# Head norm and gate of the RWKV half, and the first block of the output projection: roots and reciprocals in columns

## The reference, cut to what matters

```
def rwkv_output(y, f, lp):
    mean = jnp.mean(y, axis=-1, keepdims=True)              # over the 64 channels of a head
    var = jnp.mean(jnp.square(y - mean), axis=-1, keepdims=True)
    yn = ((y - mean) * lax.rsqrt(var + GN_EPS)).reshape(y.shape[:2] + (RWKV_WIDTH,))
    yn = yn * lp['ln_w'] + lp['ln_b']
    bonus = sum(jnp.sum(f['r'] * kd * lp['rk'], axis=-1, keepdims=True) * f['v'] for kd in f['k'])
    return (yn + bonus.reshape(yn.shape)) * f['gate']       # f['gate'] = sigmoid(g) @ g2
...
out_l = jnp.concatenate([att_l, rw_l.astype(att_l.dtype)], axis=-1) @ lp['w_out']
```

## Time and profile before

| what | value |
|---|---|
| median of 3 executions | 1767.23 us (1766.62 to 1778.11) |
| profiled execution, its own time | 1766.91 us |
| its span, first to last instruction | 1765.1 us |
| mean granted TensorE clock | 0.942 of full speed |
| PE busy | 1607.1 us (91%) |
| DVE, ACT, POOL busy | 715.8, 569.9, 860.7 us (41%, 32%, 49%) |

### The profile page before, as it was taken

The page is one execution under the profiler, slowest core; times in us unless marked ns, Lnnn a source line. Parts: engine busy times, 40 slices in busy tenths (PEclk is TensorE's granted clock), DMA queues, the critical chain, the costliest instruction groups (busy, mean ns, idle before and its releaser), DMA issues. The chain is left out here.

```text
span 1765.1 us, 35427 instructions
## 1 busy us (share of the span) xinstructions
PE 1607.1 (91%) x15584; PEld 1321.9 (75%) x15584; DVE 715.8 (41%) x1060; ACT 569.9 (32%) x816; POOL 860.7 (49%) x399
## 2 busy tenths in 40 slices
PE   5899999588888886789999999999989899999996
PEld 2688878467676784678888888888867688888885
DVE  2343256667686755652121212640194521212135
ACT  3424245543435323233232313032221432323230
POOL 1432100296867741526778888834442344444441
PEclk9999999788999998889999999969999799999998
DMA  8321100031312221223444444212221122222221
GB/s 324 131 73 48 57 1 1 1 112 62 122 52 99 75 76 57 70 72 119 145 146 148 149 148 145 95 48 95 95 95 48 48 95 96 96 95 95 95 95 48
DMA packets 23617, 162.15 MB, mean 92 GB/s; under 512 B 2624, under 2 KB 3264, under 8 KB 4800
## 3 DMA queue, kind: packets, MB, share of 16 engines
q1 hardware_dynamic: 21904, 154.09, 24.4%
q10 hardware_dynamic: 1584, 6.13, 0.9%
HBM read 157.71 MB, written 2.10 MB: 91 GB/s over the span
## 5 line engine op out<-in xcount | busy, mean ns | idle before, releaser
L221 POOL TENSOR_TENSOR v<-raw,v 128x1024 fp32r<-128x1024 f32 x160 | 388.3, 2448 | 422.3 <-ACT v L209 397.9
L238 PE MATMUL bank<-hm,v 128*128 128x512 f32 x2112 | 488.2, 393 | 7.9 <-DVE hm L1852 5.4
L238 PEld LDWEIGHTS bank<-hm,v 128*128 128x128 f32 x2112 | 399.3, 190 | 97.1 <-issue 10.6
L238 PE MATMUL bank<-hid,v 128*128 128x512 f32 x1536 | 349.5, 389 | 0.0
L238 PEld LDWEIGHTS bank<-hid,v 128*128 128x128 f32 x1536 | 288.3, 188 | 59.9
L209 ACT ACTIVATE v<-raw 128x2048 fp32r<-128x2048 f32 x77 | 147.5, 1916 | 421.0 <-PE bank L238 420.9
L1983 DVE TENSOR_TENSOR bank<-bank,rl 128x512 f32<-128x512 f32 x64 | 44.8, 700 | 275.2 <-ACT rl L1962 275.2
L221 POOL TENSOR_TENSOR w<-raw,w 128x1024 fp32r<-128x1024 f32 x22 | 54.1, 2478 | 136.2 <-ACT w L209 136.2
L937 POOL TENSOR_TENSOR raw<-raw,cs 128x2048 f32<-128x2048 f32 x24 | 87.6, 3650 | 52.1 <-DVE at L1383 52.1
L511 PE MATMUL bank<-h,w 128*128 128x512 f32 x600 | 109.3, 344 | 0.0
L511 PEld LDWEIGHTS bank<-h,w 128*128 128x128 f32 x600 | 94.0, 191 | 14.3 <-issue 0.3
(11 more groups left out here) (288 smaller groups left out, 2349.3 us busy)
## 6 DMA issues: line engine op xcount, KB each, us to landing
raw<-w_in SPq DMA_DIRECT2D x119, 1024.0 KB, 4.8
mraw<-wm_in SPq DMA_DIRECT2D x16, 1024.0 KB, 4.8
raw<-wm_in SPq DMA_DIRECT2D x3, 1024.0 KB, 16.3
xres<-x_in ACTq DMA_DIRECT2D x1, 2048.0 KB, 8.2
yb<-wm_in SPq DMA_DIRECT2D x2, 1024.0 KB, 19.5
mixed_in<-wm_in SPq DMA_DIRECT2D x2, 1024.0 KB, 23.3
xres<-x_in SPq DMA_DIRECT2D x1, 2048.0 KB, 7.5
out_T<-xres ACTq DMA_DIRECT2D x8, 256.0 KB, 2.0
```

What stands on the lines that cost most here:

```text
L221: i = nc.gpsimd.tensor_tensor(W[1][n % 2][:, k:k + 4], raw[n % 2][:, k:k + 4], W[0][n % 2][:, k:k + 4].bitcast(F32), SUB)
L238: last = nc.tensor.matmul(bank(b(s, m), 0, hi - lo), W[w][s][:, k, m * P:(m + 1) * P], H[h][:, k, lo:hi], start=(k == 0 and w == h == 0), ...
```

## The change

- The sums of squares are made per token in columns: for each pair and each group of 128 tokens, the squares are the stationary operand and two columns of onesh the moving one. 16 such matmuls write a 128x32 piece of PSUM, gsum (tokens on partitions). One ACT root and one DVE reciprocal of 128x32 follow, ginv.
- ginv is spread back over the channels by 32 matmuls of 64 stationary columns (a broadcast column of ginv) with the identity as moving operand, 8 per pair, two halves of 64 output partitions.
- The gate's matmuls stand before the sums of squares. DVE multiplies weight and gate into the centred values (yg) and offset and gate into the bonus (in vT) beforehand, and afterwards does one product and one sum per pair. The ACT step L1588 is gone.
- g2 is loaded at the end of the block before, behind the load of x, and lies in a buffer of its own.
- ACT makes W[0] of block 35 and h[0] of the attention half first in the block; W[0] of block 36 follows the root.
- W[1] of block 36 is made by DVE, in one instruction after its last sum, and no longer by POOL.
- The product of block 35 goes over k outside and the two tiles m inside.

```diff
...
+    g2 = sb(drw, "g2", [P, PAIRS * P])
...
             sp.dma_start(x[:], A["x"]).then_inc(x_back, 16)
+            sp.dma_start(g2[:], A["g2"]).then_inc(g2_in, 16)
...
-                for i in range(PAIRS):
-                    pe.wait_ge(gsq_ready, i + 1)
-                    nc.tensor.matmul(bank(i), K("onesh"), sq[i % 2][:], start=True, stop=True).then_inc(var_done, 1)
                 pe.wait_ge(g2_in, 16)
                 for i in range(PAIRS):
                     nc.tensor.matmul(bank(4 + i), g2[:, i * P:(i + 1) * P], gT[:], start=True, stop=True)\
                         .then_inc(gate_done, 1)
-
-                pe.wait_ge(root_ready, PAIRS)
-                pe_block(pe, S_OUT, W, h, parts=one,
-                         ready=lambda k: (lo_made, max(1, k - PAIRS + 2)))
+                for i in range(PAIRS):
+                    pe.wait_ge(gsq_ready, i + 1)
+                    for g in range(TG):
+                        at = 2 * (i * TG + g)
+                        last = nc.tensor.matmul(gsum[:, at:at + 2], sq[i][:, g * P:(g + 1) * P], K("onesh")[:, ::HD],
+                                                start=True, stop=True)
+                last.then_inc(gsum_done, 1)
+                pe.wait_ge(ginv_ready, 1)
+                for i in range(PAIRS):
+                    if i >= 2:
+                        pe.wait_ge(gated, 2 * (i - 1))
+                    for g in range(TG):
+                        for e in range(2):
+                            last = nc.tensor.matmul(spread_at[i][e * HD:(e + 1) * HD, g * P:(g + 1) * P],
+                                                    ginv[:, i * TG + g, e:e + 1].to_broadcast([P, HD]), K("ident"),
+                                                    start=True, stop=True)
+                    last.then_inc(spread_done, 1)
+
+                s = S_OUT % 2
+                pe.wait_ge(split_ready[s], nth(S_OUT))
...
+                for k in range(KT):
+                    pe.wait_ge(lo_made, max(1, k - PAIRS + 2))
+                    for m in range(2):
+                        for w, e in ((0, 0), (0, 1), (1, 0)):
+                            last = nc.tensor.matmul(bank(2 * s + m), W[w][s][:, k, m * P:(m + 1) * P], h[e][:, k, :],
+                                                    start=k == w == e == 0, stop=(k == KT - 1 and w == 1))
...
             def _(act):
+                act_hi(act, S_OUT, W)
+                nc.scalar.activation(h[0][:, 0:PAIRS, :], attT, ACT.Copy).then_inc(hi_made, 1)
                 for i in range(PAIRS):
                     act.wait_ge(yc_ready, i + 1)
...
+                    nc.scalar.activation(sq[i][:], rT[:, i, :], ACT.Square).then_inc(gsq_ready, 1)
+                act.wait_ge(gsum_done, 1)
+                nc.scalar.activation(flat, gsum, ACT.Sqrt, bias=small[:, 1:2], scale=1.0 / HD).then_inc(root_ready, 1)
                 act_hi(act, S_OUT + 1, W)
...
             def _(dve):
...
+                    nc.vector.scalar_tensor_tensor(yg[i][:], rT[:, i, :], R("lnw", i, i + 1), bank(4 + i), MUL, MUL)\
+                        .then_inc(gated, 1)
+                    nc.vector.scalar_tensor_tensor(vT[:, i, C:N], vT[:, i, C:N], R("lnb", i, i + 1), bank(4 + i), ADD, MUL)\
+                        .then_inc(gated, 1)
+                    if i == 2:
+                        dve.wait_ge(root_ready, 1)
+                        nc.vector.reciprocal(flat, flat).then_inc(ginv_ready, 1)
+                dve.wait_ge(gsq_ready, PAIRS)
+                for i in range(PAIRS + 1):
+                    if i < PAIRS:
+                        dve.wait_ge(spread_done, i + 1)
+                        dve.wait_ge(gated, 2 * i + 2)
+                        nc.vector.tensor_tensor(spread_at[i], spread_at[i], yg[i][:], MUL).then_inc(yn_ready, 1)
+                    if i:
+                        dve.wait_ge(yn_ready, i)
+                        nc.vector.tensor_tensor(rT[:, i - 1, :], spread_at[i - 1], vT[:, i - 1, C:N], ADD)\
+                            .then_inc(o_ready, 1)
+                dve.wait_ge(hi_ready[(S_OUT + 1) % 2], nth(S_OUT + 1))
+                s = (S_OUT + 1) % 2
+                nc.vector.tensor_tensor(W[1][s][:], raw[s][:], W[0][s][:].bitcast(F32), SUB).then_inc(split_ready[s], 1)
...
             def _(pool):
...
-                pool_lo(pool, S_OUT + 1, W)
```

More of the change, by code:

```diff
@@ L1539, in build @@
     with ExitStack() as st:
[L1540 to L1546, removed]
+        sq, yg = ([sb(st, f"{name}{i}", [P, T]) for i in range(PAIRS)] for name in ("gsq", "yg"))
+        ginv = sb(st, "ginv", [P, PAIRS * TG, 2])
+        flat = ginv[:].rearrange("p g h -> p (g h)")
+        S = sems(top, "mean_done", "yc_ready", "gsq_ready", "gsum_done", "root_ready", "ginv_ready", "gate_done", "gated",
+                 "spread_done", "yn_ready", "o_ready", "hi_made", "lo_made")
+        (mean_done, yc_ready, gsq_ready, gsum_done, root_ready, ginv_ready, gate_done, gated, spread_done, yn_ready,
+         o_ready, hi_made, lo_made) = S
+        gsum = bank(0, 0, 2 * PAIRS * TG)
+        spread_at = [bank(i) for i in (0, 1, 4, 5)]
         with nc.Block() as block:
@@ new lines, in _ @@
+                s = S_OUT % 2
+                pe.wait_ge(split_ready[s], nth(S_OUT))
+                for m in range(2):
+                    pe.wait_ge(tile_free[s][m], nth(S_OUT) - 1)
+                for k in range(KT):
+                    pe.wait_ge(lo_made, max(1, k - PAIRS + 2))
+                    for m in range(2):
+                        for w, e in ((0, 0), (0, 1), (1, 0)):
+                            last = nc.tensor.matmul(bank(2 * s + m), W[w][s][:, k, m * P:(m + 1) * P], h[e][:, k, :],
+                                                    start=k == w == e == 0, stop=(k == KT - 1 and w == 1))
+                        if k == KT - 1:
+                            last.then_inc(tile_done[s][m], 1)
@@ L1571, in _ @@
             @block.scalar
             def _(act):
+                act_hi(act, S_OUT, W)
+                nc.scalar.activation(h[0][:, 0:PAIRS, :], attT, ACT.Copy).then_inc(hi_made, 1)
                 for i in range(PAIRS):
                     act.wait_ge(yc_ready, i + 1)
[L1575 to L1579, removed]
-                    nc.scalar.activation(rg[i][:], bank(i), ACT.Sqrt, bias=small[:, 1:2], scale=1.0 / HD)\
-                        .then_inc(root_ready, 1)
@@ L1583, in _ @@
-                act_hi(act, S_OUT, W)
-                nc.scalar.activation(h[0][:, 0:PAIRS, :], attT, ACT.Copy).then_inc(hi_made, 1)
+                    nc.scalar.activation(sq[i][:], rT[:, i, :], ACT.Square).then_inc(gsq_ready, 1)
+                act.wait_ge(gsum_done, 1)
+                nc.scalar.activation(flat, gsum, ACT.Sqrt, bias=small[:, 1:2], scale=1.0 / HD).then_inc(root_ready, 1)
                 act_hi(act, S_OUT + 1, W)
-                for i in range(PAIRS):
-                    act.wait_ge(yn_ready, i + 1)
-                    nc.scalar.activation(rT[:, i, :], rT[:, i, :], ACT.Identity, scale=R("lnw", i, i + 1),
-                                         bias=R("lnb", i, i + 1)).then_inc(ys_ready, 1)
```

11 lines of the change are left out of this document (2 added, 9 removed).

## The result

| what | before | after |
|---|---|---|
| median of 20 executions | 1773.12 us (1760.97 to 1778.59) | 1758.01 us (1752.63 to 1772.21) |
| ratio after / before | | 0.9932, interval 0.9911 to 0.9953 |
| profiled execution, its span | 1766.91, 1765.1 us | 1762.35, 1760.6 us |
| mean granted TensorE clock | 0.942 | 0.942 |

The forecast was 1751.2 us, in a range up to 1756.0; 1758.0 lies outside. The ratio makes the gain 1773.1 x 0.0068 = 12.1 us (8.3 to 15.8), against 16.0 forecast. The medians differ by 15.1.

A forecast was written before the change was run, and what follows sets the result against it. PE's stage was taken as a chain of waits on POOL's attention rest and DVE's reciprocals; rebuilt, it ends at 715.0 instead of 730.95, 16.0 us less: 1766.9 - 16.0 = 1750.9, plus 0.3 gives 1751.2 us, range 1748.5 to 1756.

The forecast's parts named there:

- The chain: PE's rebuilt stage from first mean to next block's first matmul: 26.8 us instead of 42.8.
- the sum: All terms of the rebuilt stage added: 16.0 us won, giving 1751.2 us; chance 0.45 as it stands.
- the table load: ACT's load before the new root, 1.28 us: put right behind the squares and hidden by 3.2 us.
- The tail: POOL's last rests and DVE's split of block 36: in time, cover at least 2.9 us; if late, 1 to 3 us.
- spread 3.6 us at full clock: 32 matmuls, 64 records on PE, after root and reciprocal: 3.6 us, bounds 3.6 and, at half clock, 7.2.
- the clock falls in the thin stretch: Rival: PE's clock falls around sums and root, 4.4 us of thin work; loses 1.9 us, giving 1753.1; chance 0.27.
- blocks 36 to 38 and everything after are moved, not changed: Code behind the stage: keeps its length, blocks 36 to 38 still running in 32.9 us.
- the base: Starting time for the sum: profiled execution 1766.9 us, with the median of the runs 0.3 above it.
- Half clock throughout: Rival: PE stays at half clock through spread and blocks 35 to 38; loses 34.3 us, giving 1785.5; chance 0.03.
- small term: Rival: exposed ACT table load costs 1.3 us, late rests or split 1 to 3, both some 4; chance 0.13.
- More than the sum: Rival: root and reciprocal take 0.6 us and work overlaps the projection's start; up to 2 us earlier, 1749.2; chance 0.12.
- the shared port: DVE's split against POOL's rests: a rest held for the whole 2.8 us comes at 712.8 against PE's 712.9, cover gone.

The follow-up runs named there:

- best_again: Second run of the changed kernel with idle matmuls in recurrence and next norm stage and gates interleaved with the sums: median 1752.09 us, ratio 0.9883, stage 25.91.
- a_again: The changed kernel once more, unchanged: median 1757.14 us, ratio 0.9932 to the kernel before, stage 28.30 with means at full clock.
- pool_split: The changed kernel with block 36's split given back from DVE to POOL, ahead of the four rests: stage 30.39 us with slow means.
- warm_norm: The changed kernel with two idle matmuls around the first column sums of the norm behind block 38: median 1757.81 us, ratio 0.9926.
- best: The changed kernel with idle matmuls in recurrence and next norm stage and gates interleaved with the sums, first run: median 1752.12 us, ratio 0.9896, stage 27.61.
- warm_tail: The changed kernel with an idle 256-column matmul behind each of the recurrence's last ten steps: median 1751.6 us, ratio 0.9905, stage 29.52.
- m_outer: The changed kernel with block 35's 48 matmuls tile by tile (m outside, k inside): stage 31.90 us with fast means, own time of one execution 1757.79.
- gate_last: The changed kernel with the fourth pair's gate matmul moved between sums and spread: median 1759.05 us, ratio 0.9946, stage 27.53.
- cols_alone: The changed kernel with ACT's two copies (block 35, attention half) back behind the root: stage 36.96 us with slow means.
- b_warm: The kernel before with idle matmuls between the recurrence's last steps: median 1769.07 us, ratio 0.9987, stage 43.54.
- b_again: The kernel before once more, unchanged: 1772.24 us in this profile, stage 44.56 with the means mostly at half clock.

## Why the prediction was wrong

**The chain held.** At every step that the sum named: no wait for g2 or the squares; 3.63 us for the sums in columns (3.6 forecast); 0.77 of idle for root and reciprocal (0.8); the table load hidden; no wait between spread and projection; 48 matmuls in 11.18 (11.0 + 0.2); 0.47 to hand over. At full clock the spread is 3.64 (3.6), which best_again shows. Put that into a_again's stage, 28.30 - 1.67 = 26.6, and it is the forecast's 26.8 within 0.2. The tail was safe too, though tighter than its 2.9 us: 2.6 us from the last rest to PE's need of it, because a rest did wait for DVE's split, as the paragraph on that feared.

**Step that failed 1: the term "spread 3.6 us at full clock".** It measured 5.31 in after, a_again, pool_split, warm_norm and best, 5.32 in warm_tail, 5.97 in m_outer and 4.57 in gate_last (in cols_alone the wait behind it hides its end): of the ten profiles that hold this spread, nine have part of it at half clock, and one doesn't. The clock falls in before's stage as well, but there a wait hides it: in b_warm the first 12 matmuls took 0.8 us more than in before (5.46 against 4.67), and the wait behind them was 0.8 shorter (3.53 against 4.31). The change takes the waits away, so after pays for its fall in full. The rival *the clock falls in the thin stretch* had the fall; I gave it 0.27 where it should have had most of the weight. That its price came out (1.9 forecast, 1.7 measured) is partly luck. It had the clock come back only some 4 us after large matmuls resume; in after and a_again it was back at 709.6 and 705.9, before the first large matmul (710.64, 707.00), after 3.4 us at half clock. Two of its readings of the earlier trace rows are off as well: 0.86 over 702 to 704 puts the fall at 703.4, not 703.7 (4.6 us after large matmuls stopped), and 0.70 over 184 to 185 puts the return at 184.6, not 184.3. My reading put the thin stretch at 4.4 us, sums and root, between two stretches after which the clock had fallen, and stopped there. But the spread is thin work as well, 64 records of 57 ns. The stretch in question was sums, root and spread, 8 us, longer than both, and the rows said so already. Its length alone doesn't fix the moment: the clock fell 2.2 us (warm_tail) to 5.4 us (pool_split) after the start of the sums, and in best 0.2 us after a gate's large matmul.

**Step that failed 2: "blocks 36 to 38 and everything after are moved, not changed".** Blocks 36 to 38 do run in 32.8 us. The norm stage behind them costs 41.2 to 43.6 us, by when the clock falls in it, and a stage moved by 14 us meets another moment. The rest of the program has two forms too. Put end to end, the four profiles of the two kernels are (us):

| profile | start of the stage | stage | blocks 36 to 38 | next stage | from there to the end |
|---|---|---|---|---|---|
| before | 688.15 | 42.80 | 32.77 | 41.36 | 960.06 |
| b_again | 691.96 | 44.56 | 32.76 | 41.32 | 959.87 |
| after | 692.09 | 30.20 | 32.77 | 43.53 | 961.97 |
| a_again | 690.35 | 28.30 | 32.76 | 43.55 | 962.03 |

Both profiles of before had the short forms and both of after the long, 2.2 us and 2.0. With them the profiles' account is 14.4 - 2.2 - 2.0 = 10.2 us, inside the ratio's 8.3 to 15.8, and below its middle, 12.1. b_warm shows both long forms with before's code, pool_split and m_outer, with after's, have something between in the next stage and the short form behind it. How often each kernel has which form isn't known from one or two profiles. So that the next stage's length goes with the clock is shown; that this change gave back 2.2 or 4.2 us in the mean is only argued.

**Step that failed 3: the base.** I set the sum against one execution of 1766.9 and a median of three, 1767.2, and added nothing to the range for it. The three ran from 1766.6 to 1778.1; the median of twenty is 1773.1, 5.9 above. By the medians this is the largest part of the miss: forecast 1751.2, measured 1758.0, 6.8 apart, of which the base has 5.9 and the gain 0.9. With that base and the sum as it was, the forecast would have been 1757.1. By the means of the same twenty, 1771.6 and 1759.6, whose quotient is the ratio, the forecast is about 8.3 too low, 4.4 by the base and 3.9 by the gain. In the three later timings the median of before was 1768.9, 1771.1 and 1771.0. So the base was too low by all of them, by 1.7 to 5.9 us, but whether it or the gain weighs more isn't settled. As a ratio the forecast said 0.9909 (1751.2 / 1767.2), just outside the measured 0.9911 to 0.9953: that part is the gain. Steps 1 and 2 have 1.7 + 2.2 + 2.0 = 5.9 us in these profiles, more than the 3.9 missing by the ratio, whose interval reaches that far.

**The other rivals.** Half clock throughout did not happen: the clock was back 4.3 us after the spread began. Its price was read too low: of the 12 matmuls in 4.67 us only the first 3.6 us were at half clock. In b_warm twelve at half clock took 5.46, 0.46 each, so 0.23 more than at full clock and not 0.16:

```profile
710.62 5.46 PE L238 MATMUL bank<-ho,wo 128*128 128x512 f32 x12 [11.18 <-POOL ho L1616]
```

No small term was exposed. More than the sum did not happen in after; the stage of best_again, 25.91, has the full clock in the spread (3.64) and gates between its sums; what the gates give by themselves was not measured.

On the shared port, the forecast had left open whether a long DVE operation holds POOL back. It does. After: three rests in 5.89 while the split ran, first rest 1.30; in pool_split, with no such split, 1.28 each. One rest bears all of it: it took 3.36, from 713.18 to 716.54, and ended 1.16 after the split, which ended at 715.38. In cols_alone the split met POOL's attention rest, which ended at 718.70; it took 5.25 from 715.59 on, so it ended 2.14 after that rest, and then POOL's four rests took 7.20 instead of 5.11. After's 2.49 holds a short wait of this kind too: POOL's rest before it ended at 713.23, 2.15 before the split. So each waits for the other's whole instruction, in both directions. The Trainium skill, SBUF — State Buffer, section SBUF: two separate sides, has it so: the first to start holds the port pair for its whole instruction, and the other fully blocks; the runs agree.

## What to carry to other kernels

When two waits stand one behind the other, removing either alone pays little: here 4.0 and 7.6, together 14.4. When a stage is rebuilt out of small matmuls, count everything thin in one row, with the work behind the last wait included, before pricing it at full clock; and put the base of a forecast, and its range, on the spread of the executions shown and not on the profiled one. A kernel whose clock falls and rises many times can take two to four microseconds more or less far behind the change (here 2.4 in the next stage and some 2 behind it), which a single profile can't tell from the change itself.

## What the runs showed of the hardware that was not expected

- PE's small matmuls at full clock: 32 records of two columns in 3.63 us, 64 records of 128 columns with 64 stationary ones in 3.64. The spread behind the sums had part of it at 1.2 GHz in nine profiles of ten (in three of the ten with gates' large matmuls between).
- Large matmuls put into the thin stretch (gate_last, best) did not keep the clock up reliably: in best it fell in one profile and not in the other.
- The same norm stage takes 41.2 to 43.6 us without a change to its code (eleven profiles), by when in it the clock first falls.
- The recurrence's last small steps leave the means at 1.2 GHz in some executions (5.1 to 5.6 us instead of 3.5), in both kernels; idle matmuls between the steps gave fast means in all four profiles that have them, against five of ten without, and steps of 1.03 us instead of 1.27, with no delay of the steps to be seen.
- DVE's split with two SBUF inputs, 128x2048, ends 2.15 us after the POOL instruction that holds it, and a POOL rest that meets it ends 1.16 after the split.
